# An encoder block on eight cores: six buffers for normalized rows, later x loads, and the last norm product split over two engines

## The chip, the cores and the metric

The kernel runs on all 8 cores of one Trainium2 chip. Each core computes one of the 8 sequences of the batch; nothing is exchanged between them. Cores 0 to 3 lie on one die, 4 to 7 on the other. The metric is the device time in microseconds (us) of the slowest core. Each core has a matrix engine (TensorE, PE), a vector engine (VectorE, DVE), ScalarE (ACT) and GpSimd (POOL); SyncE (SP) issues transfers. 16 DMA engines carry out what SP, ACT and POOL issue. Each engine takes its instructions in order, and semaphores order the engines among each other.

## The reference

What is computed, for one sequence of 2048 rows of 1024 (16 meta rows are put in front for the mixers):

```python
u = rmsnorm(h, norm1_g)
q, c, iq, ik, iw, pv, gates = split(u @ w_in)
attn = sparse_attention(...)            # top-256 keys of a chunk-causal indexer, shared latent
pool = multiscale_pool(pv, w_pool, pool_scale)
g_attn, g_pool = split(sigmoid(gates))
merged = g_attn * (attn @ w_branch_attn) + g_pool * (pool @ w_branch_pool)
h = h + merged @ w_out
u = rmsnorm(h, norm2_g)
h = h + hier_moe(u)                     # top-1 of 4 groups, top-2 of its 8 experts, hidden 256
out = rmsnorm(h, final_norm_g)          # meta rows dropped
```

The change is in the last three lines' surroundings: `h + merged @ w_out`, the second norm, and the last line.

## The kernel before

The program records each operation with the buffers it reads and writes (`pg.op`, `pg.dma`), and from these works out the semaphore waits; within an engine the order is that in which the code is written. The rows are cut into 16 tiles of 128 (`NT`). A tile of h is `hacc[:, j, :]`, 128 partitions of 1024 float32, in SBUF for the rest of the program.

Stages in order of time on the profiled core: projections and the indexer with sparse attention (to about 790 us), the branch products and gates giving `mergedT` (to 968), the **join stage** (968 to about 1076, with routing to 1098), the **expert stage** (to 1370), and the **final stage** (to the end). A barrier stands ahead of the join stage, none between it and the end of the final stage.

*Join stage.* Tiles are walked in the order `walk`: 12 to 15, 8 to 11, 0 to 7; t counts places in this walk. x of tiles 12 to 15 is loaded a stage earlier. At the start SP issues the gain, the routing constants, the twelve other x tiles (`load_x`) and the weights of experts 0 and 1 (`load_w`). In step t the code writes:

- `scale_rows(t-1)`: a reciprocal on DVE, then the norm product into a bf16 buffer `xn2[k]`. For even t-1 it is one DVE instruction (L1335). For odd it is a scaling on ACT (L1339) and a product with the gain on POOL (L1341).
- `join(t)`: twice 8 matmuls (L1314) into one of three PSUM banks, each followed by an add of x on DVE (L1319), then square and sum (L1323) and square root (L1325) on ACT.
- `flip(t-2)`: a write of `xn2[k]` to the table `u_rows` in device memory, issued by ACT; eight transpositions on PE (L1351) into a bank of their own, and a copy on ACT (L1355).
- `score_rows(t-3)`: eight small matmuls (L1364) and an add on DVE (L1368) give the router's logits. From t = 11 on, each step takes six operations of the first half's routing besides, nearly all on DVE.

There are two `xn2` buffers, in arena R0. The buffers `xg` for gathered rows (six of the same size, arena R2) are set to zero by POOL before the walk; in the expert stage `pull(i)` gathers rows of `u_rows` into them, leaving out rows whose index is out of bounds. The expert stage keeps four buffers of expert weights filled ahead of itself.

*Final stage.* `fetch(j)` brings two expert outputs per row (1 MB, SP), eight tiles ahead. `merge(j)` adds them to `hacc` with two DVE instructions (L1689) and takes square and root on ACT (L1692, L1695). `leave(j-1)` then takes the reciprocal on DVE (L1701), multiplies with reciprocal and gain on DVE (L1703) into one of six buffers `ofin`, and issues the output from ACT. Since `fetch(0)` to `fetch(7)` all claim the old buffers of the expert stage (list `moe`), the first `leave`, which claims them too, waits for the eighth fetch.

Of the kernel before, what the change touches and what calls it, by code (L numbers as in the profile page):

```python
# [9 lines left out]
BF16 = mybir.dt.bfloat16  # L10
ALU = mybir.AluOpType
AF = mybir.ActivationFunctionType
AX = mybir.AxisListType

P = 128
D = 1024
KC = 8
NT = 16
# [33 lines left out]
class Prog:  # L52
# [11 lines left out]
    def B(self, *key):  # L64
        b = self.bufs.get(key)
        if b is None:
            b = Buf(key)
            self.bufs[key] = b
        return b
# [191 lines left out]
def build(debug=None):  # L261
# [8 lines left out]
    x_d = din("x", [TX, D])  # L270
# [32 lines left out]
    pg = Prog(nc)  # L303
    B = pg.B

    with ExitStack() as es:
# [29 lines left out]
        def carve_at(nm, off, dtype, shape):  # L336
            save = cursor[nm]
            cursor[nm] = off
            ap = carve(nm, dtype, shape)
            assert (off + 63) // 64 * 64 == off  # L340
            cursor[nm] = save
            return ap
# [5 lines left out]
        banks_bf = [b.bitcast(BF16) for b in banks]  # L348
        PB = [B('psum', i) for i in range(8)]
# [3 lines left out]
        gbc = [carve('R0', F32, [P, D]) for _ in range(2)]  # L353
# [125 lines left out]
        for j in tiles:  # L479
            rows = 16 if j < 0 else 128  # L480
            col0 = 0 if j < 0 else 16 + 128 * j
            k = nxt('xt4', [0, 1, 2, 3])
# [236 lines left out]
        if stop_after >= 4:  # L719
# [11 lines left out]
            for m in range(4):  # L731
                bk = nxt('gen', allb)
                pg.op('pe', lambda e, bk=bk, m=m: e.transpose(
                    out=banks_bf[bk][:, 0:128], in_=wuk_bf[:, m * 128:(m + 1) * 128], identity=ident_bf),
                    reads=[B('wuk_bf'), B('ident_bf')], writes=[PB[bk]])
                for hp in range(2):
                    h = 2 * m + hp
                    pg.op('dve', lambda e, bk=bk, h=h, hp=hp: e.tensor_copy(
                        out=ukT_pad[64 * hp:64 * hp + 64, h, :], in_=banks_bf[bk][64 * hp:64 * hp + 64, 0:128]),
                        reads=[PB[bk], B('ukT_pad')], writes=[B('ukT_pad', h)])  # L740
# [434 lines left out]
        if run_tail:  # L1175
# [7 lines left out]
            for grp in range(4):  # L1183
# [57 lines left out]
        rstd2 = carve('R2', F32, [P, NT])  # L1241
# [10 lines left out]
        idx_s = carve('R2', I32, [P, 48])  # L1252
        wbuf = [carve_at('R0', 0, BF16, [P, 6144]), carve_at('R0', 12288, BF16, [P, 6144]),
                carve_at('R2', 16384, BF16, [P, 6144]), carve_at('R0', xt_off, BF16, [P, 6144])]
        xn2 = [carve_at('R0', 24576 + 2048 * i, BF16, [P, D]) for i in range(2)]
        uTs = [carve_at('R0', 28672 + 2048 * i, BF16, [P, KC, 128]) for i in range(2)]
        t32 = carve_at('R0', junk_off, F32, [P, D])
        sqj = carve_at('R3', 32768, BF16, [P, D])
# [24 lines left out]
        def load_w(x_):  # L1283
            load_gu_w(x_)
            load_d_w(x_)

        def load_x(j):
            pg.dma('sp', hacc[:, j, :], x_d[128 * j:128 * (j + 1), :], writes=[B('hacc', j, 0), B('hacc', j, 1)])

        if run_tail:  # L1290
            pg.dma('sp', gbc[1], g2_d.partition_broadcast(128), writes=[B('gbc', 1)])
            pg.dma('sp', rconst, croute_d, writes=[B('rconst')])
            for j in list(range(8, 12)) + list(range(0, 8)):
                load_x(j)
            load_w(0)
            load_w(1)
            for i in range(2):
                for q in range(3):
                    pg.op('pool', lambda e, i=i, q=q: e.memset(xg[i][q], 0.0), writes=[B('xg', i, q)])
            pg.op('pool', lambda e: e.tensor_copy(out=tri_bf, in_=rconst[:, 0:128]), reads=[B('rconst')], writes=[B('tri')])  # L1300
            pg.op('pool', lambda e: e.memset(ones_m, 1.0), writes=[B('ones_m')])
            pg.op('pool', lambda e: e.tensor_copy(out=iota_bf, in_=rconst[:, 128:384]), reads=[B('rconst')], writes=[B('iota')])
# [24 lines left out]
                      reads=[B('ssq', j), B('eps')], writes=[B('rs', j)])  # L1327

            def scale_rows(t):
                j, k = walk[t], t % 2  # L1330
                hb = [B('hacc', j, 0), B('hacc', j, 1)]
                pg.op('dve', lambda e: e.reciprocal(out=rstd2[:, j:j + 1], in_=rstd2[:, j:j + 1]),
                      reads=[B('rs', j)], writes=[B('rs', j)])
                if t % 2 == 0:
                    pg.op('dve', lambda e: e.scalar_tensor_tensor(  # L1335
                        out=xn2[k], in0=hacc[:, j, :], scalar=rstd2[:, j:j + 1], in1=gbc[1], op0=ALU.mult, op1=ALU.mult),
                        reads=hb + [B('rs', j), B('gbc', 1)], writes=[B('xn2', k)])
                else:
                    pg.op('act', lambda e: e.activation(out=t32, in_=hacc[:, j, :], func=AF.Identity, scale=rstd2[:, j:j + 1]),  # L1339
                          reads=hb + [B('rs', j)], writes=[B('t32')])  # L1340
                    pg.op('pool', lambda e: e.tensor_tensor(out=xn2[k], in0=t32, in1=gbc[1], op=ALU.mult),  # L1341
                          reads=[B('t32'), B('gbc', 1)], writes=[B('xn2', k)])

            def flip(t):
                j, k = walk[t], t % 2
                pg.dma('act', urow_d[128 * j:128 * (j + 1), :], xn2[k], reads=[B('xn2', k)], writes=[B('u_row', j)])

                def tps(e):
                    last = None
                    for kc in range(KC):  # L1350
                        last = e.transpose(out=banks_bf[TPB][:, kc * 128:(kc + 1) * 128],  # L1351
                                           in_=xn2[k].rearrange("t (p k) -> t k p", k=KC)[:, kc, :], identity=ident_bf)
                    return last
                pg.op('pe', tps, reads=[B('xn2', k), B('ident_bf')], writes=[PB[TPB]])
                pg.op('act', lambda e: e.copy(out=uTs[k], in_=banks_bf[TPB][:, 0:1024].rearrange("p (a b) -> p a b", a=KC)),  # L1355
                      reads=[PB[TPB]], writes=[B('uTs', k)])

            def score_rows(t):
                j, k = walk[t], t % 2
# [136 lines left out]
            for t in range(NT + 4):  # L1496
                if 1 <= t < NT + 1:
                    scale_rows(t - 1)
                if t < NT:
                    join(t)  # L1500
                if 2 <= t < NT + 2:
                    flip(t - 2)
                if 3 <= t < NT + 3:
                    score_rows(t - 3)
                if t >= NH + 3:
                    for _ in range(6):
                        if first_half:
                            first_half.pop(0)()
# [51 lines left out]
        def pull(i):  # L1560
            for q, col in ((0, 2 * i), (1, 2 * i + 1), (2, 32 + i)):
                pg.gather(xg[i % 2][q], urow_d, idx_g[:, col:col + 1], TX - 1,
                          reads=[B('idx_g')] + urows, writes=[B('xg', i % 2, q)])
        pull(0)
        pull(1)
        pg.branch_on(flag[0:1, 0:1], [B('flag')])
# [1 line left out]
        silm = [carve_at('R0', 24576 + 1536 * i, F32, [P, 2 * CAP]) for i in range(3)]  # L1568
        xTm = [carve_at('R3', 3072 * i, BF16, [P, KC, CAP]) for i in range(4)]
        ysb = [carve_at('R3', 12288 + 4096 * i, F32, [P, D]) for i in range(5)]  # L1570
        early = [B('xn2', k) for k in range(2)] + [B('uTs', k) for k in range(2)]
        late_r3 = [B('R3a')]

        def turn(i):
# [124 lines left out]
        def leave(j):  # L1699
            s = j % 6  # L1700
            pg.op('dve', lambda e: e.reciprocal(out=rstd2[:, j:j + 1], in_=rstd2[:, j:j + 1]),  # L1701
                  reads=[B('rs', j)], writes=[B('rs', j)])
            pg.op('dve', lambda e: e.scalar_tensor_tensor(  # L1703
                out=ofin[s], in0=hacc[:, j, :], scalar=rstd2[:, j:j + 1], in1=gbc[0], op0=ALU.mult, op1=ALU.mult),
                reads=[B('hacc', j, 0), B('hacc', j, 1), B('rs', j), B('gbc', 0)],
                writes=[B('ofin', s)] + (moe if j < 6 else []))
            pg.dma('act', out_d[128 * j:128 * (j + 1), :], ofin[s], reads=[B('ofin', s)], writes=[B('out', j)])

        for j in range(8):
# [203 lines left out]
```

How the kernel before makes its waits and increments, by code:

```python
        def stream(ename, h, ops, base, n):  # L209
            info = parts[n][1]
            for i, o in enumerate(ops):
                for t in o.waits:
                    if t[0] == 'c':
                        h.wait_ge(esem[t[1]], signo[n][t[1]][t[2]])
                    else:
                        s, val = info[t[1]]
                        h.wait_ge(dsem[s], val)
                if o.fn is None:
                    continue
                inst = o.fn(h)
                if o.dma is not None:
                    inst.then_inc(dsem[info[o.dma][0]], 16)
                elif base + i in signo[n][ename]:
                    inst.then_inc(esem[ename], 1)
```

## Time and profile before

| | us |
|---|---|
| median of 3 runs (lowest, highest) | 1492.72 (1492.47, 1503.7) |
| the profiled execution | 1493.79 |
| its span, core 7 | 1492.2 |
| span of the other cores | 1452.1 to 1488.1 |
| busy in the span: PE, DVE, ACT, POOL | 1066.1, 879.3, 738.9, 305.6 |

The span is the time from the first to the last instruction of the profiled core. The page's chain that ended last gives PE 45%, DVE 18%, ACT 8% and DMA 8% of it. A line such as L122, L125 or L130 is that of a helper that issues transfers; names such as R are the SBUF arenas, ps is PSUM, and `ACTq` or `SPq` marks the issue of a transfer on that engine's queue. A bracket in the timeline tells how long the engine was idle before an instruction and what released it.

### The profile page before, as it was taken

The page shows a single profiled execution, that of the slowest core. Times are in us where ns is not written, and L with a number is a line of the kernel's source. Part 1 is how long each engine was busy: PE and PEld are TensorE (multiplying, and loading weights), DVE is VectorE, ACT ScalarE, POOL GpSimd, SP SyncE. Part 2 cuts the span into 40 slices and gives each one's busy share as a digit, 9 for nine tenths or more (in the row PEclk, how much of TensorE's full clock was granted, in tenths as well). Part 3 has the DMA queues.
Part 4 walks back from the last instruction along what each step waited for, and adds up shares of the span by engine and source line. Part 5 has one row for each costly group of instructions (what it writes and reads, how often), then busy time and mean ns, then how long its engine had stood idle before and what let it go on. Part 6 is the DMA issues. An engine that isn't in the chain of part 4 may idle for free.

```text
span 1492.2 us, 23009 instructions; the slowest of 8 cores (1452.1 to 1492.2 us)
## 1 busy us (share of the span) xinstructions
PE 1066.1 (71%) x6606; PEld 546.1 (37%) x6606; DVE 879.3 (59%) x1812; ACT 738.9 (50%) x1387; POOL 305.6 (20%) x316
## 2 busy tenths in 40 slices
PE   2589667788888889999848999968547777776000
PEld 1345223333333334444423444424334544453000
DVE  3434699899999999999811344334632322322186
ACT  5733656677777778888743222235313323332132
POOL 2025402122121212221221000022123333332000
PEclk9999577889999999999988999989759998899555
DMA  9402554575868679999676220081237889985592
GB/s 195 113 1 29 63 58 58 71 97 74 97 72 98 81 83 108 112 105 104 90 97 136 30 29 1 1 296 50 85 109 247 274 270 293 288 297 174 190 350 107
DMA packets 76322, 187.73 MB, mean 126 GB/s; under 512 B 18792, under 2 KB 30568, under 8 KB 72096
## 3 DMA queue, kind: packets, MB, share of 16 engines
q0 software_dynamic: 51264, 87.55, 39.6%
q1 hardware_dynamic: 20320, 86.05, 18.8%
q10 hardware_dynamic: 4608, 12.58, 2.1%
q8 instruction: 59, 0.97, 0.3%
q14 instruction: 71, 0.58, 0.1%
HBM read 223.33 MB, written 88.08 MB: 209 GB/s over the span
## 4 chain that ended last, share of the span: by engine, by line
PE 45%; DVE 18%; issue 14%; ACT 8%; DMA 8%; another core or an unknown queue 3%; POOL 2%; DVEq 0%; ACTq 0%; SPq 0%; POOLq 0%
DVE R L961 9%; PE ps L1214 7%; PE ps L1608 5%; PE ps L1632 4%; DMA R<-y_rows 3%; PE ps L823 3%; PE ps L1020 2%; PE ps L1021 2%; PE ps L1038 2%; PE ps L1314 2%; PE ps L1039 2%; PE ps L623 2%; PE ps L1198 2%; PE ps L1206 2%
## 5 line engine op out<-in xcount | busy, mean ns | idle before, releaser
L961 DVE TENSOR_SCALAR_CACHE_REDUCE R<-R 128x272 bf16<-128x272 f32 (+14 forms) x240 | 342.2, 1426 | 11.6 <-DVE R L961 0.5
L1024 ACT ACTIVATE R<-ps,R 128x512 bf16<-128x512 f32 x304 | 209.1, 690 | 70.4 <-PE ps L1021 63.8
L813 ACT ACTIVATE R<-ps 128x400 bf16<-128x400 f32 (+14 forms) x352 | 159.3, 512 | 55.0 <-PE ps L808 53.5
L1038 PE MATMUL ps<-R 128*128 128x512 bf16 x304 | 120.2, 395 | 36.1 <-ACT R L1046 34.4
L1050 POOL TENSOR_TENSOR R<-R 128x512 bf16<-128x512 f32 x32 | 40.6, 1270 | 455.6 <-ACT R L1048 357.7
L1020 PE MATMUL ps<-R 128*128 128x512 bf16 x304 | 121.2, 399 | 7.4 <-DVE R L928 3.9
L823 PE MATMUL ps<-R 128*128 128x400 bf16 (+14 forms) x352 | 105.7, 379 | 26.1 <-POOL R L796 16.4
L1021 PE MATMUL ps<-R 128*128 128x512 bf16 x304 | 120.7, 397 | 0.0
L1039 PE MATMUL ps<-R 128*128 128x512 bf16 x304 | 120.2, 395 | 0.0
L1214 PE MATMUL ps<-R 128*128 128x512 bf16 x512 | 116.9, 382 | 0.0
L808 PE MATMUL ps<-R 32*128 32x400 bf16 (+14 forms) x352 | 71.9, 370 | 30.9 <-DVE R L928 14.9
L1632 PE MATMUL ps<-R 128*128 128x512 bf16 (+1 forms) x256 | 85.1, 448 | 11.6 <-ACT R L1641 9.3
L1608 PE MATMUL ps<-R 128*128 128x192 bf16 x1024 | 92.0, 249 | 0.7 <-DVE R L1594 0.7
L1608 PEld LDWEIGHTS ps<-R 128*128 128x128 bf16 x1024 | 84.7, 99 | 15.7 <-issue 15.4
L1615 DVE TENSOR_TENSOR R<-R,ps 128x384 bf16<-128x384 f32 x32 | 17.7, 555 | 109.7 <-remote 51.4
L130 POOL DMA_INDIRECT y_rows<-R x48 | 47.6, 992 | 161.9 <-DVE R L1644 64.7
L1226 DVE TENSOR_TENSOR R<-R,ps 128x512 f32<-128x512 f32 x32 | 22.0, 688 | 94.1 <-ACT R L1222 94.1
L1582 PE MATMUL ps<-R 128*128 128x128 bf16 x384 | 32.3, 240 | 61.7 <-ACT R L1590 52.0
L1214 PEld LDWEIGHTS ps<-R 128*128 128x128 bf16 x512 | 50.5, 99 | 61.6 <-issue 2.1
L1314 PE MATMUL ps<-R 128*128 128x512 bf16 x256 | 63.0, 402 | 10.5 <-DVE R L1319 8.1
L1641 ACT COPY R<-ps 128x512 f32<-128x512 f32 x64 | 37.3, 582 | 65.1 <-PE ps L1632 63.2
L1644 DVE COPY R<-ps 128x512 f32<-128x512 f32 x64 | 44.1, 690 | 42.0 <-PE ps L1632 40.9
(210 smaller groups left out, 1854.3 us busy)
## 6 DMA issues: line engine op xcount, KB each, us to landing
R<-expert_bf SPq DMA_DIRECT2D x32, 1024.0 KB
R<-x SPq DMA_DIRECT2D x32, 512.0 KB
expert_bf<-w_eg POOLq DMA_DIRECT2D x32, 512.0 KB, 12.1
expert_bf<-w_eu POOLq DMA_DIRECT2D x32, 512.0 KB
expert_bf<-w_ed POOLq DMA_DIRECT2D x32, 512.0 KB
R<-expert_bf SPq DMA_DIRECT2D x32, 512.0 KB
R<-y_rows SPq DMA_DIRECT2D x16, 1024.0 KB
out<-R ACTq DMA_DIRECT2D x16, 512.0 KB, 5.2
```

What stands on the lines that cost most here:

```text
L813: pg.op('act', lambda e, bx=bx, ri=ri: e.activation(out=rbuf[ri][:, 0:n], in_=banks[bx][:, 0:n], func=AF.Relu), reads=[PB[bx]], writes=[B( ...
L823: pg.op('pe', lambda e, h=h, ri=ri: e.matmul(banks[PSS][:, 0:n], lhsT=dg[:, h, :], rhs=rbuf[ri][:, 0:n], start=(h == 0), stop=(h == 7)), r ...
L961: pg.op('dve', lambda e: e.tensor_scalar(out=junkbf[:, 0:S], in0=sc[:, 0:S], scalar1=mids[:, n_ - 1:n_], scalar2=None, op0=ALU.is_ge, op1= ...
L1020: e.matmul(banks[bl][:, 0:512], lhsT=cnT[:, kc0:kc0 + 128], rhs=qrhs, start=True, stop=False)
L1021: return e.matmul(banks[bl][:, 0:512], lhsT=ident_bf, rhs=mrow, start=False, stop=True)
L1024: pg.op('act', lambda e: e.activation(out=pT[pi], in_=banks[bl][:, 0:512], func=AF.Exp, scale=ATTN_SCALE, bias=negsh[:, par:par + 1]), rea ...
L1038: e.matmul(banks[bO][:, 0:512], lhsT=ckeys[:, i, 0:128], rhs=pT[pi], start=first, stop=last_)
L1039: return e.matmul(banks[bS][:, 0:512], lhsT=ones_bf, rhs=pT[pi], start=first, stop=last_)
L1214: last = e.matmul(banks[bk][:, 0:512], lhsT=wt[:, kc, n4 * 128:(n4 + 1) * 128], rhs=uT[:, kc, c0:c0 + 512], start=(kc == 0), stop=(kc == K ...
L1314: last = e.matmul(banks[bk][:, 0:512], lhsT=mergedT[:, nn, 128 * j:128 * (j + 1)], rhs=w_out[:, nn, 512 * hh:512 * (hh + 1)], start=(nn == ...
L1608: last = e.matmul(banks[bk][:, CAP * fh:CAP * (fh + 1)], lhsT=w[:, c_:c_ + 128], rhs=xt_[:, kc, :], start=(kc == 0), stop=(kc == KC - 1))
L1632: last = e.matmul(banks[bk][lo:hi_, 0:512], lhsT=hd[:, f, t0:t1_], rhs=w[:, 4096 + 1024 * f + 512 * hh:4096 + 1024 * f + 512 * (hh + 1)], ...
```

## The change

In the join stage `xn2` becomes six buffers, which are the six `xg` buffers; their memsets are gone, and the first two `pull`s list the `xn2` buffers as written. Of x, only tiles 8 and 9 are asked for at the start. The others are asked for one at a time, tile `walk[t + 6]` once the first add of tile `walk[t]` is done; the weights of experts 0 and 1 are asked for in steps 6 and 9. In the final stage, the norm product of odd tiles becomes a scaling on ACT and a product in place on POOL.

```diff
-        xn2 = [carve_at('R0', 24576 + 2048 * i, BF16, [P, D]) for i in range(2)]
+        xn2 = [xg[i // 3][i % 3] for i in range(6)]
@@
-        def load_x(j):
-            pg.dma('sp', hacc[:, j, :], x_d[128 * j:128 * (j + 1), :], writes=[B('hacc', j, 0), B('hacc', j, 1)])
+        def load_x(j, after=()):
+            pg.dma('sp', hacc[:, j, :], x_d[128 * j:128 * (j + 1), :], reads=list(after), writes=[B('hacc', j, 0), B('hacc', j, 1)])
@@
-            for j in list(range(8, 12)) + list(range(0, 8)):
+            for j in range(8, 10):
                 load_x(j)
-            load_w(0)
-            load_w(1)
-            for i in range(2):
-                for q in range(3):
-                    pg.op('pool', lambda e, i=i, q=q: e.memset(xg[i][q], 0.0), writes=[B('xg', i, q)])
@@ scale_rows
-                j, k = walk[t], t % 2
+                j, k = walk[t], t % 6
@@ flip (uTs, the copy's target, stays at two buffers: ku)
-                j, k = walk[t], t % 2
+                j, k, ku = walk[t], t % 6, t % 2
@@ the walk
                     join(t)
+                    if t + 6 < NT:
+                        load_x(walk[t + 6], [B('hacc', walk[t], 0)])
+                    if t in (6, 9):
+                        load_w(t // 3 - 2)
@@ pull
-                          reads=[B('idx_g')] + urows, writes=[B('xg', i % 2, q)])
+                          reads=[B('idx_g')] + urows, writes=[B('xg', i % 2, q)] + ([B('xn2', 3 * i + q)] if i < 2 else []))
@@
-        early = [B('xn2', k) for k in range(2)] + [B('uTs', k) for k in range(2)]
+        early = [B('uTs', k) for k in range(2)]
@@ leave
-            pg.op('dve', lambda e: e.scalar_tensor_tensor(
-                out=ofin[s], in0=hacc[:, j, :], scalar=rstd2[:, j:j + 1], in1=gbc[0], op0=ALU.mult, op1=ALU.mult),
-                reads=[B('hacc', j, 0), B('hacc', j, 1), B('rs', j), B('gbc', 0)],
-                writes=[B('ofin', s)] + (moe if j < 6 else []))
+            hb = [B('hacc', j, 0), B('hacc', j, 1)]
+            al = moe if j < 6 else []
+            if j % 2 == 0:
+                pg.op('dve', lambda e: e.scalar_tensor_tensor(
+                    out=ofin[s], in0=hacc[:, j, :], scalar=rstd2[:, j:j + 1], in1=gbc[0], op0=ALU.mult, op1=ALU.mult),
+                    reads=hb + [B('rs', j), B('gbc', 0)], writes=[B('ofin', s)] + al)
+            else:
+                pg.op('act', lambda e: e.activation(out=ofin[s], in_=hacc[:, j, :], func=AF.Identity, scale=rstd2[:, j:j + 1]),
+                      reads=hb + [B('rs', j)], writes=[B('ofin', s)] + al)
+                pg.op('pool', lambda e: e.tensor_tensor(out=ofin[s], in0=ofin[s], in1=gbc[0], op=ALU.mult),
+                      reads=[B('ofin', s), B('gbc', 0)], writes=[B('ofin', s)])
```

Lines behind the removed ones have numbers lower by five, and in the final stage by one: L1319 becomes L1314, L1335 becomes L1330, L1692 becomes L1691.

The order on SP's queue at the start of the join stage. `expert_bf` are the weights in pairs of a 1 MB and a 0.5 MB load:

```order
 L122 DMA R<-c_route 128x560
-L122 DMA R<-x 128x1024 x12
+L122 DMA R<-x 128x1024 x9
 L122 DMA R<-expert_bf 128x4096
 L122 DMA R<-expert_bf 128x2048
+L122 DMA R<-x 128x1024 x3
 L122 DMA R<-expert_bf 128x4096
 L122 DMA R<-expert_bf 128x2048
```

Three x loads (for t = 7, 8, 9) now stand behind the weights of expert 0; which of the others wait for an add is not in these rows.

ScalarE's order in the final stage, from the square of tile 2 on. First the kernel before: L1692 is the square, L1695 the root.

```order
L1692 ACTIVATE R<-R 128x1024
L1695 ACTIVATE R<-R 128x1
L122 DMA out<-R 128x1024
L1692 ACTIVATE R<-R 128x1024
L1695 ACTIVATE R<-R 128x1
```

And the kernel changed, from the same place (L1691 is the square, L1694 the root, L1709 the new scaling of tile 1):

```order
L1691 ACTIVATE R<-R 128x1024
L1694 ACTIVATE R<-R 128x1
L1709 ACTIVATE R<-R 128x1024
L122 DMA out<-R 128x1024
L1691 ACTIVATE R<-R 128x1024
L1694 ACTIVATE R<-R 128x1
L122 DMA out<-R 128x1024
```

The scaling stands between a tile's root and the previous tile's output issue, in every second step; the last one stands alone ahead of the last issue. GpSimd's order, at the start of the join stage and at the end of the program:

```order
-L1299 MEMSET R 128x1024 x6
-L1300 CAST R<-R 128x128
-L1301 MEMSET R 128x128
-L1302 CAST R<-R 128x256
-L1341 TENSOR_TENSOR R<-R 128x1024 x8
+L1295 CAST R<-R 128x128
+L1296 MEMSET R 128x128
+L1297 CAST R<-R 128x256
+L1336 TENSOR_TENSOR R<-R 128x1024 x8
...
 L130 DMA y_rows<-R 4096x1024 x11
+L1711 TENSOR_TENSOR R<-R 128x1024 x8
```

Six memsets are gone, and eight products are new behind the last scatter.

## Rows read from the trace of the kernel before

**Rows 1.** Busy time by stretch (length; engines busy; PE clock, DMA share, GB/s).

```profile
982.40:994.70 12.30, 4.38 (x33) 2.02 (x30) 2.16 (x4) 2.06 (x4) 2.03 (x1) 0.85 1.01 319
...
1008.00:1023.80 15.80, 14.28 (x102) 7.14 (x99) 7.08 (x15) 9.25 (x14) 2.38 (x1) 0.89 0.14 51
...
1419.70:1480.00 60.30, 0.00 (x0) 0.00 (x0) 56.43 (x59) 20.21 (x42) 0.00 (x0) 0.50 0.73 261
```

**Rows 2.** Timeline, the first stall: start, duration, engine, line [idle before <-releaser].

```profile
983.26 0.38 ACTq L122 DMA_DIRECT2D u_rows<-R  x1
...
985.73 1.89 PE L1314 MATMUL ps<-R 128*128 128x512 bf16 x8
992.70 1.28 DVE L1335 SCALAR_TENSOR_TENSOR R<-R 128x1024 bf16<-128x1024 f32 x1 [8.89 <-DMA u_rows<-R]
...
994.73 3.36 PE L1314 MATMUL ps<-R 128*128 128x512 bf16 x8 [7.12 <-DVE R L1319]
...
1004.43 2.34 POOL L1341 TENSOR_TENSOR R<-R 128x1024 bf16<-128x1024 f32 x1 [20.00 <-DMA u_rows<-R]
...
1006.91 1.05 PE L1351 MATMUL ps<-R 128*128 128x128 bf16 x8 [4.41 <-POOL R L1341]
...
1013.82 3.61 PE L1314 MATMUL ps<-R 128*128 128x512 bf16 x16
```

**Rows 3.** Timeline, a later stretch of the join stage.

```profile
1023.83 3.61 PE L1314 MATMUL ps<-R 128*128 128x512 bf16 x16
...
1027.35 1.28 DVE L1335 SCALAR_TENSOR_TENSOR R<-R 128x1024 bf16<-128x1024 f32 x1 [1.65 <-DMA u_rows<-R]
...
1032.81 0.68 PE L1351 MATMUL ps<-R 128*128 128x128 bf16 x8 [1.22 <-ACT R L1355]
...
1043.36 3.61 PE L1314 MATMUL ps<-R 128*128 128x512 bf16 x16
...
1047.51 3.69 PE L1314 MATMUL ps<-R 128*128 128x512 bf16 x16
```

**Rows 4.** Timeline of GpSimd and VectorE, late in the join stage.

```profile
1053.98 2.35 POOL L1341 TENSOR_TENSOR R<-R 128x1024 bf16<-128x1024 f32 x1 [7.61 <-ACT R L1339]
1054.23 2.71 DVE L1436 TENSOR_TENSOR R<-R 128x256 f32<-128x256 f32 x2
...
1057.05 0.43 DVE L1439 TENSOR_TENSOR R<-R 128x256 bf16<-128x256 f32 x1
```

**Rows 5.** Timeline of GpSimd and VectorE, early in the program.

```profile
126.26 2.30 DVE L652 SCALAR_TENSOR_TENSOR R<-R 128x2057 bf16<-128x2057 f32 x1 [2.23 <-POOL R L645]
128.48 1.85 DVE L656 TENSOR_TENSOR R<-R 128x7 f32<-128x7 f32 x1
...
127.31 3.00 POOL L639 TENSOR_TENSOR R<-R 128x1023 f32<-128x1023 f32 x1
...
135.47 1.89 POOL L639 TENSOR_TENSOR R<-R 128x1023 f32<-128x1023 f32 x1 [0.21 <-POOL R L645]
```

**Rows 6.** Timeline of the final stage, first tiles and last issues.

```profile
1419.67 1.28 DVE L1703 SCALAR_TENSOR_TENSOR R<-R 128x1024 f32<-128x1024 f32 x1 [31.45 <-DMA R<-y_rows]
1420.87 2.67 DVE L1689 SCALAR_TENSOR_TENSOR R<-R 128x1024 f32<-128x1024 f32 x2
...
1423.63 1.06 ACT L1692 ACTIVATE R<-R 128x1024 bf16<-128x1024 f32 x1 [33.85 <-DVE R L1701]
1423.72 1.28 DVE L1703 SCALAR_TENSOR_TENSOR R<-R 128x1024 f32<-128x1024 f32 x1
...
1424.88 0.29 ACT L1695 ACTIVATE R<-R 128x1 f32<-128x1 f32 x1
...
1477.69 2.16 ACTq L122 DMA_DIRECT2D out<-R  x2
```

**Rows 7.** Two ScalarE lines: count, min/median/max in ns, first and last start.

```profile
L1339 ACT ACTIVATE R<-R x8: 1149/1153/1159, 980.8 to 1067.7; 128x1024 f32<-128x1024 f32 x8
...
L1355 ACT COPY R<-ps x16: 1005/1012/1012, 983.7 to 1074.4; 128x1024 bf16<-128x1024 bf16 x16
```

More of the change, by code:

```diff
@@ L1354, in flip @@
                 pg.op('pe', tps, reads=[B('xn2', k), B('ident_bf')], writes=[PB[TPB]])
-                pg.op('act', lambda e: e.copy(out=uTs[k], in_=banks_bf[TPB][:, 0:1024].rearrange("p (a b) -> p a b", a=KC)),
-                      reads=[PB[TPB]], writes=[B('uTs', k)])
+                pg.op('act', lambda e: e.copy(out=uTs[ku], in_=banks_bf[TPB][:, 0:1024].rearrange("p (a b) -> p a b", a=KC)),
+                      reads=[PB[TPB]], writes=[B('uTs', ku)])
             def score_rows(t):
```

## The prediction

> **What bounds the kernel now.** I read the stage windows first, then the timeline of core 7 (the slowest, and the one profiled) in the two stages that the change touches, then what each wait there was released by. Times are microseconds from the span's start.
>
> The join stage runs from 968.6 to about 1076 and has two regimes. While x and the first weights are streaming in, the 16 DMA engines are full: their share is 1.01 in 982.4 to 994.7, against 0.14 in 1008.0 to 1023.8 [rows 1]. In that flood the first write of normalized rows is issued at 983.26, and the norm product of tile 2 (L1335), which needs the same buffer back, starts only at 992.70, after 8.89 of idle time. The vector engine runs in order, so the adds that free PSUM banks stand behind it, and TensorE stops for 7.12. The GpSimd product of tile 3 waits in the same way until 1004.43, and TensorE waits another 4.41 for it, then runs its next eight matmuls cold (3.36 for eight, against 1.89 before) [rows 2]. After 1008 the write lands sooner, but each even product still waits 1.65, and it passes the delay on by way of the ScalarE copy to TensorE (1.22); two pairs of tiles take from 1023.83 to 1043.36, so 9.77 a pair [rows 3].
>
> The final stage is bound by the vector engine: 56.43 busy of 60.3 [rows 1]. Its cycle for one tile is two merges (2.67 with their gap), a reciprocal and the norm product (1.28); the products of neighbouring tiles start at 1419.67 and 1423.72, so 4.05 a tile. ScalarE needs only 1.54 a tile there, from 1423.63 to the end of the square root at 1425.17, and GpSimd nothing [rows 6]. The chain begins at 1419.67 because the first product waits for the eighth fetch; the change leaves that wait alone, since tile 0 is even and keeps its place and its list of old buffers.
>
> **Part one: six buffers, x asked for late, no memsets.** The six memsets are GpSimd work ahead of its first product and nobody waits for them: 0. Six buffers remove the wait for the write from two tiles back, at all places. What comes next in line I worked out from tile 4 on. Its matmuls start at 985.73 as before. Product 2 runs at 983.8 instead of 992.7, so the adds of tile 3 are done at 986.4 and tile 4 ends at 989.2. From there the slowest loop goes through ScalarE: square and root 1.54 [rows 6], issue 0.38 [rows 2], copy 1.01 and, for odd tiles, the scaling 1.15 [rows 7], where a transposition waits for the previous copy. A product on GpSimd takes 2.35 [rows 4] and also holds up the even tile's vector product for about 0.6. This gives tile 5 at 990.5, tile 6 at 995.1 and tile 7 at 1000.0, against 1013.82 in the trace [rows 2]: 13.8 gained. From there a pair costs 4.55 plus 4.65, 9.2 instead of 9.77, over two and a half pairs 1.4. From tile 11 on the vector engine is filled by the routing steps of the first half, and no more of the pace comes through; but it reaches that section one removed wait of 1.65 earlier, less what the slower chain takes, which I put at 1.3. **Sum of part one: 16.5 gained.** The lower bound takes the early stalls alone without the cold matmuls, less a ScalarE loop that is a little longer than I think: 12. The upper bound is TensorE's own pace, 4.15 a tile as between 1043.36 and 1047.51 where it waited for nothing [rows 3], from tile 4 to 11: about 20.
>
> The x loads are costed at nothing. A load now goes out when the add of the tile six places ahead is done, so it has 6 times 4.6, or 27.6, before its own add. The first write under a full queue took 9.4 (983.26 to 992.70) [rows 2]. Behind the load at step 6 stand 1.5 MB of expert weights and at step 9 again 1.5 MB; at the 319 GB/s of the full window [rows 1] that is 4.7 for a load that stands behind them. If that cover were gone, the adds, and so PSUM, would wait.
>
> **Part two: the last product split.** For odd tiles the vector engine loses 1.28 less overlap, 1.20. In exchange ScalarE gets 1.15 [rows 7] and GpSimd 2.35, and the output's issue on ScalarE's queue now waits for GpSimd. Queued behind it are the next tile's square and root, on which the next reciprocal depends.
>
> What decides is whether the two engines can run side by side. In the trace they can't when both read two SBUF operands. GpSimd's product of 2.35 starts at 1053.98; a pair of vector TENSOR_TENSORs of 256 columns (0.43 each alone) starts at 1054.23 and takes 2.71 [rows 4]. The first ended only once GpSimd was done. The other way round, a SCALAR_TENSOR_TENSOR runs from 126.26 to 128.56, and a GpSimd TENSOR_TENSOR that starts at 127.31 takes 3.00, where the same form takes 1.89 alone. The vector instruction of seven columns queued next took 1.85, up to GpSimd's end [rows 5]. So each blocks the other, and a waiting GpSimd instruction gets its turn ahead of the vector engine's next one. The merges and products of the final stage are all of the form that blocks. The Trainium skill says the same (SBUF — State Buffer, "Who interferes with whom"): a vector instruction with two SBUF inputs contends with a GpSimd one that reads SBUF, and the loser blocks fully. By that rule a split of this kind adds GpSimd's time to the vector engine's; without it, it would take 1.20 off every second tile. The trace agrees with the rule.
>
> A pair of tiles is then, on the vector engine, 8.1 - 1.2 + 2.2 = 9.1 (2.2 and not 2.35, since a blocked vector instruction gets going some 0.15 before GpSimd's printed end). ScalarE's chain in a pair is 1.54 + 0.1 + 1.15 + 0.1 + 2.35 + 0.1 + 0.4 + 1.54 + 0.4 = 7.7, which fits in 9.1. From the first merge of tile 2 (1420.87 in the trace) to the issue of the last output there are now six pairs of 9.1, so 54.6, and a last one of about 14.8: two merges end 5.4 in, GpSimd's product 13 runs from 5.6 or 6.9, the output issue, square and root of tile 15 come after it (about 10.7), then reciprocal, scaling 1.15, product 2.35 and issue. That is 69.4. The trace has 58.6, to the second issue at about 1479.5 [rows 6]. **Sum of part two: 10.8 lost**, with bounds of 8 (GpSimd's turn partly in gaps) and 12.5.
>
> The 8 and 12.5 assume that GpSimd with float32 output takes 2.35, as with bf16 output. The row of 1.89 is float32 to float32 [rows 5], so nothing speaks for much more.
>
> **Sum.** 16.5 gained and 10.8 lost make 5.7 gained. The profiled execution took 1493.79 (span 1492.2), the median of the runs is 1492.72, a difference of 1.1 that I leave aside. 1492.7 - 5.7 = **1487.0**. What follows the last output's issue is untouched, and the expert stage between the two changed ones shifts as a whole.
>
> **Rivals.**
> - *No mutual blocking in the final stage.* Then the pair is bound by ScalarE's chain, 7.7: six of them and a last one of 14.1 make 60.3, still 1.7 more than the trace, because the last tile is odd and its longer way lies open. The net is 14.8 gained: 1478. For it speaks only that no row shows this exact pair of forms with both at 1024 columns. Chance 0.06.
> - *GpSimd is starved.* If the vector engine's instructions leave no gap, GpSimd comes only when the vector engine waits for the root behind the blocked issue. Then a pair costs 6.9 + 2.35 + 0.45 + 1.54, 11.2, or 3.1 more than now; seven of these and the tail of 2.3 lose 24, net 7.5 lost: 1500. It decides if GpSimd loses more than two turns in a pair. Against it stands the row of 127.31, where it got in at once. Chance 0.04.
> - *x late.* If loads need over 27.6, the gain of part one goes and part two stays: 1503. It needs three times the longest landing in the rows. Chance 0.04.
> - *Part one pays more*, because ScalarE's loop is shorter than worked out: 20 gained and 9 to 10.8 lost, 1482. Chance 0.10.
> - The forecast itself, 1487, with its own range of 1481 to 1493: chance 0.76.
>
> **How the numbers follow.** The forecast and the case of a better part one hold 0.86. To reach 8 in 10 with the uncertainty of both bounds I take the edge of the first rival and a little over the forecast's own upper end: 1478 to 1495. A change of under 1% (14.9) is about what a measurement of this kernel can't tell from none. Faster by more needs the first rival or both lucky bounds: 0.09. Slower by more than 1% needs starvation or late x at their worst: 0.04. The rest is 0.87.
>
> **What would show it.** In the profile after: no wait of a product for a u_rows write; TensorE's stalls of 7.12 and 4.41 gone; the stage from its first matmul to the last logits add some 16 shorter. In the final stage vector rows of about 3.5 instead of 1.28 wherever GpSimd's product runs, a pair of 9.1, and about 70 from tile 2's merge to the last issue. It would be wrong if the GpSimd rows and the vector rows overlap at full length, if the scaling on ScalarE waits for something other than its reciprocal, or if adds wait for x.

## The result

The changed kernel takes 1479.27 us (median of 4 runs, 1476.2 to 1482.97), the kernel before 1492.6; the ratio is 0.990, 95% interval 0.9853 to 0.9946. The forecast was 5.7 gained, the profiled executions differ by 10.8 (1493.79 to 1482.97), the medians by 13.3. So the sign and the place were right, and the size was about half of what came. Medians, ratios and intervals, here and below, leave out the executions in which the cores of one die ran at a lower clock and finished some per cent later.

The profile after is again that of core 7, span 1481.4. On that core, between fixed points of the program:

| stretch on core 7, us | before | after | forecast change | measured change |
|---|---|---|---|---|
| start to first matmul of the join stage | 968.6 | 968.6 | 0 | 0 |
| join stage and routing (to the last cast of the router) | 129.3 | 110.9 | -16.5 | -18.4 |
| from there to the first product of the final stage | 321.8 | 321.3 | 0 | -0.5 |
| first product of the final stage to the end | 72.5 | 80.6 | +10.8 | +8.1 |
| span | 1492.2 | 1481.4 | -5.7 | -10.8 |

The same two stretches on all eight cores: join and routing 125.8 to 131.8 before, 110.9 to 111.6 after; the final stage 72.5 to 72.8 before and 80.6 on every core after.

The last row ends with a closing stretch, from the landing of the last output to the end of the span. It is the same on all eight cores of a kernel, within 0.05, and differs between kernels; why is open: 10.1 before, 9.9 after, and 8.5 to 10.5 in the kernels below. The program does no computing in it, so the final stage is also read from its first product to the issue of the last output: 59.8 before, 68.0 after, 8.2 more, on every core.

First the join stage. In the windows of the changed kernel (columns as in [rows 1]) the engines that stood still in the same stretch are at work, at full clock, and the DMA engines carry their load evenly:

```profile
982.40:994.70 12.30, 11.12 (x90) 5.97 (x88) 7.30 (x13) 7.87 (x13) 4.34 (x2) 1.00 0.59 191
994.70:1008.00 13.30, 12.95 (x98) 6.82 (x97) 7.30 (x16) 9.46 (x15) 2.35 (x1) 1.00 0.82 273
```

TensorE is busy for 11.12 of 12.30, where it was 4.38 [rows 1]. The timeline of the changed kernel from tile 4 on:

```profile
983.23 0.35 ACTq L122 DMA_DIRECT2D u_rows<-R  x1
...
983.88 1.59 DVE L1330 SCALAR_TENSOR_TENSOR R<-R 128x1024 bf16<-128x1024 f32 x1
...
985.67 3.61 PE L1309 MATMUL ps<-R 128*128 128x512 bf16 x16
...
989.65 0.69 PE L1346 MATMUL ps<-R 128*128 128x128 bf16 x8 [0.37 <-ACT R L1350]
...
999.05 3.61 PE L1309 MATMUL ps<-R 128*128 128x512 bf16 x16
...
1003.20 3.61 PE L1309 MATMUL ps<-R 128*128 128x512 bf16 x16
...
1007.72 3.61 PE L1309 MATMUL ps<-R 128*128 128x512 bf16 x16
```

Product 2 starts at 983.88, where it started at 992.70 [rows 2]. Tile 7 starts at 999.05 instead of 1013.82 [rows 2]. From there tiles follow in 4.15 and 4.52, a pair in 8.67, where it was 9.77 [rows 3]. What is left of waiting is a few tenths for ScalarE's copy.

Now the final stage of the changed kernel, from its first product to the last issue:

```profile
1400.82 1.28 DVE L1705 SCALAR_TENSOR_TENSOR R<-R 128x1024 f32<-128x1024 f32 x1 [32.12 <-DMA R<-y_rows]
1402.02 2.67 DVE L1688 SCALAR_TENSOR_TENSOR R<-R 128x1024 f32<-128x1024 f32 x2
...
1406.22 1.13 ACT L1709 ACTIVATE R<-R 128x1024 f32<-128x1024 f32 x1
...
1407.50 2.33 POOL L1711 TENSOR_TENSOR R<-R 128x1024 f32<-128x1024 f32 x1 [57.11 <-ACT R L1709]
1407.53 3.40 DVE L1705 SCALAR_TENSOR_TENSOR R<-R 128x1024 f32<-128x1024 f32 x1
1409.91 0.34 ACTq L122 DMA_DIRECT2D out<-R  x1
1410.36 1.06 ACT L1691 ACTIVATE R<-R 128x1024 bf16<-128x1024 f32 x1 [3.01 <-POOL R L1711]
1410.84 2.66 DVE L1688 SCALAR_TENSOR_TENSOR R<-R 128x1024 f32<-128x1024 f32 x2
...
1416.32 2.34 POOL L1711 TENSOR_TENSOR R<-R 128x1024 f32<-128x1024 f32 x1 [6.48 <-ACT R L1709]
...
1454.92 2.66 DVE L1688 SCALAR_TENSOR_TENSOR R<-R 128x1024 f32<-128x1024 f32 x2
...
1466.44 2.34 POOL L1711 TENSOR_TENSOR R<-R 128x1024 f32<-128x1024 f32 x1 [3.71 <-ACT R L1709]
1468.86 0.34 ACTq L122 DMA_DIRECT2D out<-R  x1
```

The even tile's product, 1.28 alone, takes 3.40 when GpSimd's product has started 0.03 before it, and ends 1.1 after GpSimd's end: this is what it would do if it did its own work only then. A pair takes 8.82 (GpSimd from 1407.50 to 1416.32), where two tiles took 8.1 [rows 6]. From the merge of tile 2 at 1402.02 to the last issue at 1468.86 it is 66.8, against 58.6.

### The profile page after: what moved, and what is told of

It reads as the page before. It is cut to its first block, busy times and chain, and to the rows that moved or that the text cites. A ratio compares the mean times of both kernels' runs of the same rounds, so it can differ in the third digit from the quotient of the medians.

```text
span 1481.4 us, 23028 instructions; the slowest of 8 cores (1438.8 to 1481.4 us)
## 1 busy us (share of the span) xinstructions
PE 1064.9 (72%) x6606; PEld 549.1 (37%) x6606; DVE 886.1 (60%) x1804; ACT 748.1 (50%) x1395; POOL 318.1 (21%) x318
## 4 chain that ended last, share of the span: by engine, by line
PE 42%; DVE 21%; issue 15%; ACT 8%; DMA 7%; another core or an unknown queue 3%; POOL 1%; DVEq 0%; ACTq 0%; SPq 0%; POOLq 0%
DVE R L961 11%; PE ps L1214 8%; PE ps L1607 5%; PE ps L1631 4%; DMA R<-y_rows 3%; PE ps L1309 2%; PE ps L623 2%; PE ps L823 2%; PE ps L1198 2%; PE ps L1206 2%; PE ps L1038 2%; PE ps L1020 2%; PE ps L1021 2%; PE ps L1039 2%
## 5 line engine op out<-in xcount | busy, mean ns | idle before, releaser
L1038 PE MATMUL ps<-R 128*128 128x512 bf16 x304 | 120.9, 398 | 33.5 <-ACT R L1046 32.3
L1020 PE MATMUL ps<-R 128*128 128x512 bf16 x304 | 122.1, 401 | 6.4 <-DVE R L928 3.0
L1021 PE MATMUL ps<-R 128*128 128x512 bf16 x304 | 121.3, 399 | 0.0
L1039 PE MATMUL ps<-R 128*128 128x512 bf16 x304 | 120.4, 396 | 0.0
L1214 PE MATMUL ps<-R 128*128 128x512 bf16 x512 | 116.7, 381 | 0.0
L1631 PE MATMUL ps<-R 128*128 128x512 bf16 (+1 forms) x256 | 81.3, 433 | 11.7 <-ACT R L1640 10.2
L1222 ACT ACTIVATE R<-ps 128x512 f32<-128x512 f32 x32 | 19.1, 597 | 88.8 <-PE ps L1214 88.8
```

Of the source, the lines that this page charges most:

```text
L1020: e.matmul(banks[bl][:, 0:512], lhsT=cnT[:, kc0:kc0 + 128], rhs=qrhs, start=True, stop=False)
L1021: return e.matmul(banks[bl][:, 0:512], lhsT=ident_bf, rhs=mrow, start=False, stop=True)
L1038: e.matmul(banks[bO][:, 0:512], lhsT=ckeys[:, i, 0:128], rhs=pT[pi], start=first, stop=last_)
L1039: return e.matmul(banks[bS][:, 0:512], lhsT=ones_bf, rhs=pT[pi], start=first, stop=last_)
L1214: last = e.matmul(banks[bk][:, 0:512], lhsT=wt[:, kc, n4 * 128:(n4 + 1) * 128], rhs=uT[:, kc, c0:c0 + 512], start=(kc == 0), stop=(kc == K ...
L1631: last = e.matmul(banks[bk][lo:hi_, 0:512], lhsT=hd[:, f, t0:t1_], rhs=w[:, 4096 + 1024 * f + 512 * hh:4096 + 1024 * f + 512 * (hh + 1)], ...
```

## The experiments

In the tables of this section "join" is the stretch from the first matmul of the join stage to the end of routing, "final" that from the first product of the final stage to the end, and "to the last issue" that from the same product to the issue of the last output; where no core is named, the mean of the eight is given. Whole times scatter by several us between executions, so the stretches carry most verdicts. The kernels ran in three groups, each on a chip of its own, with the kernel before beside them: first the two halves, six buffers and late loads (before: 1492.07), then write-only, bystander and early claims (1487.91), then three buffers and late weights (1504.65, a single execution). Ratios are to the kernel before of the same group.

**The halves apart.** The join-only kernel keeps the old product in the final stage, the other one keeps the old join stage:

```diff
 e1_join_only: the changed kernel, but in leave
-            if j % 2 == 0: ... else: ... (the split)
+            pg.op('dve', lambda e: e.scalar_tensor_tensor(out=ofin[s], ...))
 e2_final_only: the kernel before, but in leave the split
```

> The join-stage half of the change alone (six buffers, late x, no memsets); the final stage keeps its product on the vector engine. Theory A (the two halves add up: the join stage gains 18.4 as in the trace of the changed kernel, the split product costs 8.2): the first merge of tile 2 starts near 1402, the last output issue follows 58.6 later, and the time is 1471 to 1475, faster than the changed kernel by about 8. Rival B (the split product costs nothing at the end, because the last outputs or the fetches bound the final stage anyway): the time is that of the changed kernel, 1479.

> The final-stage half alone: odd tiles scaled on ScalarE and multiplied on GpSimd, join stage as before. Theory A: 8.2 slower than the kernel before, 1500 to 1502, with a pair of tiles at 8.8 in place of 8.1 and vector products of 3.4 wherever GpSimd's runs. Rival B: within 2 of the kernel before.

The join-only kernel took 1473.44 (ratio 0.986, interval 0.9761 to 0.9959), the final-only one 1503.21 (1.007, interval 1.003 to 1.0111). Final: 73.2 and 81.2, against 72.6 before and 80.6 with the whole change. To the last issue: 60.2 and 68.05, against 59.8 and 68.0. The final-only kernel shows the same pair of rows as the changed one:

```profile
1444.89 2.34 POOL L1712 TENSOR_TENSOR R<-R 128x1024 f32<-128x1024 f32 x1 [6.48 <-ACT R L1710]
1444.91 3.41 DVE L1706 SCALAR_TENSOR_TENSOR R<-R 128x1024 f32<-128x1024 f32 x1
```

So the split costs 7.8 to 8.2 up to the last issue, wherever it stands, and rival B falls. The join-only kernel should then have been 8 faster than the changed one; it is 5.8 faster by the medians and 6 by the ratios, whose intervals overlap. Its join is 113.4, not 111.3, which accounts for the rest. On core 7 the first 40 matmuls took 10.48 in the join-only kernel (granted clock 0.85 in the first 11.7) and 8.79 in the changed one (1.00):

```profile
965.32 10.48 PE L1309 MATMUL ps<-R 128*128 128x512 bf16 x40 [2.53 <-DVE R L1230]
...
965.30:977.00 11.70, 10.74 (x42) 4.43 (x43) 3.84 (x6) 2.73 (x4) 0.77 (x3) 0.85 0.59 204
```

But that isn't the whole of it: on cores 1 to 5 of the changed kernel the first 40 took 10.48 as well, and their join is still 111.4 to 111.6. Against those the join-only kernel loses its 2 at the end of the walk. In the middle of its last tile but one TensorE waits for an add, and the last sixteen matmuls are slower. First core 7 of the join-only kernel, then core 1 of the changed one:

```profile
1030.85 1.89 PE L1309 MATMUL ps<-R 128*128 128x512 bf16 x8 [1.16 <-DVE R L1314]
...
1040.11 5.86 PE L1309 MATMUL ps<-R 128*128 128x512 bf16 x16
```

```profile
1033.40 4.86 PE L1309 MATMUL ps<-R 128*128 128x512 bf16 x16
```

The code is the same in both up to the end of routing. What shifts the late add, and why the clock falls on some cores and not on others, is open. The wait ahead of the first matmul, 2.53 in the join-only kernel and 2.43 in the changed one, doesn't decide it: cores with 10.48 and cores with 8.79 both show 2.43 in the changed kernel.

**Buffers or loads.** Two kernels take the join half apart, both with the old product at the end:

```diff
 e3_six_buffers: the join-only kernel with all loads at the start
+            for j in list(range(8, 12)) + list(range(0, 8)):
+                load_x(j)
+            load_w(0)
+            load_w(1)
 e4_late_x: the kernel before (two buffers, memsets) with the loads of the change
+                    if t + 6 < NT:
+                        load_x(walk[t + 6], [B('hacc', walk[t], 0)])
+                    if t in (6, 9):
+                        load_w(t // 3 - 2)
```

> Six buffers for normalized rows (and so no memsets), with all x loads and the weights of experts 0 and 1 asked for at the start as before; final stage as before. Theory C (the buffers carry the gain; the flooded queue then harms nobody, since a write has six tiles to land): no product waits for a write, the join stage is as short as with both, time as the join-only kernel within 2. Rival D (the late loads carry it): the writes still land 9 to 10 late and something else waits, gain under 6.

> Late x and weight loads alone, two buffers and the memsets kept; final stage as before. Theory C: the first writes land in 2 to 4 instead of 9 and the stalls of 7.1 and 4.4 on TensorE mostly go, but each even product keeps its wait of about 1.65, so the gain is 10 to 13, time 1480 to 1483. Rival D (late loads carry all of it): gain 18, 1474. Rival E (two buffers serialize at any queue length): gain under 4.

Six buffers alone took 1476.62 (0.9893, interval 0.9797 to 0.999), join 111.3: all of the gain. No product waits for a write of `u_rows` on any core, although the queue is as full as before, and although single writes took up to 10.5 to land on cores 4 to 7 and up to 20.8 on cores 0 to 3. This kernel lacks the memsets too, but they aren't what it gains by: on core 7 the first GpSimd product, behind the memsets, starts at 982.08 before and at 982.04 in the changed kernel. Late loads alone took 1490.89 (0.9987, interval 0.9944 to 1.003), join 130.5 against 128.4 before: none of it. That is where my expectation was wrong: theory C had 10 to 13 for the late loads. The first wait did shrink, but others grew in its place:

```profile
984.32 0.34 ACTq L122 DMA_DIRECT2D u_rows<-R  x1
...
987.25 1.28 DVE L1333 SCALAR_TENSOR_TENSOR R<-R 128x1024 bf16<-128x1024 f32 x1 [2.38 <-DMA u_rows<-R]
...
1006.50 2.34 POOL L1339 TENSOR_TENSOR R<-R 128x1024 bf16<-128x1024 f32 x1 [9.39 <-DMA u_rows<-R]
...
1012.70 1.28 DVE L1333 SCALAR_TENSOR_TENSOR R<-R 128x1024 bf16<-128x1024 f32 x1 [6.59 <-DMA u_rows<-R]
```

These are from core 5 of the late-loads kernel. Product 2 waits 2.38 instead of 8.89 [rows 2]. But at 1003.7 the weights of expert 0 enter the queue, and a product waits 6.59; in the kernel before, the queue was nearly empty by then (DMA share 0.14 [rows 1]) and the wait 1.65 [rows 3]. Over the stage of core 5 the vector engine's waits for writes are 19.0, where the kernel before has 16.2 on that core, and GpSimd's are 47.3 instead of 32.1.

To see whether the weights alone did this, they were put behind the walk; and to see how deep the buffers must be, the join-only kernel was run with three:

```diff
 e10_late_x_late_w: e4_late_x without its load_w in the walk
             load_w(2)   ->   load_w(0); load_w(1); load_w(2)
 e9_three_buffers: the join-only kernel
-        xn2 = [xg[i // 3][i % 3] for i in range(6)]
+        xn2 = [xg[0][i] for i in range(3)]
-                j, k = walk[t], t % 6
+                j, k = walk[t], t % 3
```

> Late x with two buffers, and the weights of experts 0 and 1 asked for only behind the walk (the late-x kernel asked for them in steps 6 and 9 and kept the stretch at 129 to 132). Theory J (the weights were the flood that kept the late-x kernel slow): the stretch falls to 116 to 122. Theory K (with two buffers a product waits for its write at any traffic; the x loads in small portions are enough): 124 to 130.

> The join-only kernel with three buffers for normalized rows instead of six (late x as in the change). Read by the stretch from the first matmul of the join stage to the end of routing: 129 before with two, 111.4 with six. Theory C (a write has one tile of 4.3 more to land than with two; writes of this stage land in 2 to 7.5 on core 5 and 7): most of it, 112 to 116. Rival: a write needs the full depth, 120 or more.

Join 126.0 without the weights (123.0 to 128.5 by core), so theory K: against late loads with the weights in the walk it is some 4 shorter, a difference between single profiled executions on two chips, and with two buffers the products wait for their writes without the weights too. With three buffers it is 114.7. The writes of `u_rows` were waited for as follows (engine and line that waited, us in all, number of waits), first on core 1 of the late-weights kernel, then on core 1 of the one with three buffers:

```profile
  POOL R L1339: 35.1, 3
  DVE R L1333: 15.6, 5
```

```profile
  DVE R L1330: 5.3, 3
```

Their single executions took 1476.12 (three buffers) and 1490.8 (late weights), against 1504.65 for the kernel before on the same chip. Three buffers with late loads carry four fifths of the gain (13.7 of 17.1), six the rest. Three buffers with all loads at the start weren't tried.

**What the final stage pays for.** In the first of two kernels GpSimd's product is replaced by work of the same length that reads nothing; it leaves out the gain of the odd tiles. In the second, GpSimd products that nobody waits for are added to the join-only kernel:

```diff
 e5_write_only: the changed kernel
-                pg.op('pool', lambda e: e.tensor_tensor(out=ofin[s], in0=ofin[s], in1=gbc[0], op=ALU.mult), ...)
+                for n in (1024, 1024, 420):
+                    pg.op('pool', lambda e, n=n: e.memset(wide[:, 0:n], 1.0), reads=[B('gbc', 0)], writes=[B('ofin', s), B('wide')])
 e8_bystander: the join-only kernel
+            if j % 2 == 1:
+                pg.op('pool', lambda e: e.tensor_tensor(out=wide, in0=gbc[0], in1=gbc[0], op=ALU.mult),
+                      reads=[B('rs', j), B('gbc', 0)], writes=[B('wide')])
```

> The changed kernel with GpSimd's product of the odd tiles replaced by three memsets of a scratch tile, 0.95 + 0.95 + 0.43 long, ordered in the same way (after ScalarE's scaling, before the output's issue). It leaves out the gain factor of the odd tiles. GpSimd then reads nothing from SBUF. Theory A (the 8 us that the final stage lost are VectorE and GpSimd excluding each other): vector products back at 1.28, a pair bound by ScalarE's chain at 7.7 instead of 8.8, final stage from its first product to the end 74 to 75 instead of 80.6. Rival F (the loss is ScalarE's queue waiting for GpSimd, exclusion is hidden behind it): pair stays at 8.8, 80.6.

> The join-only kernel with eight GpSimd products added in the final stage that nobody needs (gain times gain into a scratch tile, released by the root of each odd tile). Nobody waits for them. Theory A: each holds the vector engine up by 2.1, so a pair goes from 8.1 to 10.2 and the final stage from 72.6 to about 89. Rival F (an unneeded GpSimd product costs nothing): 72.6 to 73.2 as before.

With writes only, the final stage is 73.1 to 73.3, and the timeline of its core 6 shows the two engines side by side:

```profile
1413.76 2.59 POOL L1713 MEMSET R<- 128x1024 f32 x3 [5.09 <-ACT R L1710]
1413.79 1.28 DVE L1706 SCALAR_TENSOR_TENSOR R<-R 128x1024 f32<-128x1024 f32 x1
...
1416.43 0.34 ACTq L122 DMA_DIRECT2D out<-R  x1
1416.87 1.06 ACT L1692 ACTIVATE R<-R 128x1024 bf16<-128x1024 f32 x1 [3.28 <-POOL R L1713]
...
1418.50 0.16 DVE L1701 RECIPROCAL R<-R 128x1 f32<-128x1 f32 x1 [0.85 <-ACT R L1695]
...
1421.42 1.28 DVE L1706 SCALAR_TENSOR_TENSOR R<-R 128x1024 f32<-128x1024 f32 x1
```

The product is back at 1.28 although GpSimd has started 0.03 before it, just as in the changed kernel. The pair takes 7.63 (1413.79 to 1421.42), bound by ScalarE, whose next square waits 3.28 for GpSimd and whose root the reciprocal waits for. Final is 7.5 shorter than in the changed kernel, but 1.3 of that is the closing stretch (8.6 against 9.9). To the last issue it is 61.95 against 68.0. So of the 8.2 that the split cost, exclusion while both engines read is 6.1, and the other 2.1 is left without it: the pairs are shorter (7.6, two of them 8.0 and 8.2 on core 7), but the last tile is odd, and its longer way through ScalarE and GpSimd lies open. Without exclusion the split would still have lost that: 61.95 against 59.8 before and 60.2 in the join-only kernel. The whole time was 1473.74 (0.9902, interval 0.9866 to 0.9938).

The bystander products cost 10.0 by the whole stretch (final 83.2) and 11.8 to the last issue (72.0 against 60.2), with nobody waiting for them; whole time 1486.53 (0.996, interval 0.9931 to 0.9989). The expectation was 16. It took 2.1 for each; but this product, gain times gain, takes 1.89 and not 2.34, seven of the eight lie ahead of the last vector product, and each of them adds 1.6 to 1.7. From core 5:

```profile
1424.55 2.67 DVE L1689 SCALAR_TENSOR_TENSOR R<-R 128x1024 f32<-128x1024 f32 x2
...
1427.39 1.28 DVE L1703 SCALAR_TENSOR_TENSOR R<-R 128x1024 f32<-128x1024 f32 x1
1427.49 2.93 POOL L1708 TENSOR_TENSOR R<-R 128x1024 f32<-128x1024 f32 x1 [6.79 <-DVE R L1701]
1428.60 4.30 DVE L1689 SCALAR_TENSOR_TENSOR R<-R 128x1024 f32<-128x1024 f32 x2
```

Here the product began first, GpSimd waited 1.04 for it (2.93 instead of 1.89), and then the merge that was next in line waited for GpSimd (4.30 instead of 2.67). A waiting GpSimd instruction does get its turn ahead of the vector engine's next, as in [rows 5]. The Trainium skill (SBUF — State Buffer, "Who interferes with whom") says that such a vector instruction contends with a GpSimd one that reads SBUF and not with one that only writes it; the 3.40 of the changed kernel and the 1.28 beside memsets agree with both halves of that.

**A version that beats both.** The first product of the final stage idles for 31.45 behind the eighth fetch [rows 6], since each fetch claims all old buffers. Here the output buffers are claimed by six one-column memsets before the first fetch:

```diff
 e6_claim_early: the join-only kernel; e7_claim_early_split: the same in the changed kernel
+        for s in range(6):
+            pg.op('dve', lambda e, s=s: e.memset(ofin[s][:, 0:1], 0.0), writes=[B('ofin', s)] + moe)
         for j in range(8):
             fetch(j)
-                writes=[B('ofin', s)] + (moe if j < 6 else []))
+                writes=[B('ofin', s)])
```

> The join-only kernel, with the six output buffers claimed from the expert stage by six one-column memsets before the first fetch, so that the first product no longer waits for the eighth fetch. Theory G (fetches of 1 MB land every 5.1, and a tile of vector work is 4.05, so the final stage runs at the fetches' pace): merges and products follow each landing, the last fetch lands some 82 to 85 after the first is issued, and the end comes 15 to 25 earlier than with the join-only kernel. Rival H (output writes and fetches share the same bandwidth, 24 MB at 362 GB/s, and the wait only moved work): gain under 5.

> The same early claim in the changed kernel, so with the split product. Theory G: a pair takes 10.2 of fetching, more than the 8.8 of the split pair, so the split costs only the tail, 2 to 4 more than the kernel with the early claim alone. Rival I: the split costs its 8 here too.

With the early claim the kernel takes 1454.11 (0.9773, interval 0.9723 to 0.9824); from the first merge to the last issue it is 82.4 as a mean of the cores, where the join-only kernel has 98.2. So 15.8 come from one wait (14.9 on cores 0 to 3 alone). The timeline of its core 5:

```profile
1373.13 2.67 DVE L1688 SCALAR_TENSOR_TENSOR R<-R 128x1024 f32<-128x1024 f32 x2 [1.49 <-DMA R<-y_rows]
...
1378.43 2.67 DVE L1688 SCALAR_TENSOR_TENSOR R<-R 128x1024 f32<-128x1024 f32 x2 [1.17 <-DMA R<-y_rows]
...
1381.28 1.28 DVE L1702 SCALAR_TENSOR_TENSOR R<-R 128x1024 f32<-128x1024 f32 x1
...
1383.96 2.67 DVE L1688 SCALAR_TENSOR_TENSOR R<-R 128x1024 f32<-128x1024 f32 x2 [1.40 <-DMA R<-y_rows]
```

Merges follow the landing of their fetch, 5.3 and 5.5 apart, and products no longer wait. With the split on top it is 1471.5 (0.9877, interval 0.9802 to 0.9951), and the same stretch 88.1: the split costs 5.7 here (4.8 on cores 0 to 3), more than the tail that theory G allowed and less than rival I's 8. The traces show why. The fetches set the pace only in part of the stage. With the early claim alone the merges of tiles 8 to 12 wait for no fetch on core 3 and start 4.0 to 4.1 apart, which is the vector engine's own pace; with the split, on core 5, pairs of tiles from there on take 8.8 to 8.9.

## Why the prediction was right or wrong

- *What bounds each stage.* Right. The two TensorE stalls of 7.12 and 4.41 were waits for a write from two tiles back; six buffers alone took them away.
- *x loads late: 0.* Right as a price: no add of the changed kernel waits for x on any core. The margin was read from core 7 alone, where a write took 9.4; on cores 0 to 3 writes took up to 23.0 to land, near the cover of 27.6. As a cause it was worth nothing either: with six buffers, loads in front or late give 111.3 both. I had not separated the two in the prediction, and my later expectation of 10 to 13 for the late loads was wrong.
- *Part one, 16.5: the size was off, 18.4 came.* The step that failed is "a pair costs 4.55 plus 4.65, 9.2". It measured 8.67, of 4.15 and 4.52. The 4.15 is TensorE's own pace, so ScalarE's loop, taken as the slowest, doesn't set it: it was drawn too long. A pair thus gained 1.10 where the forecast had 0.57, or 2.8 instead of 1.4 over two and a half. Tile 7 came at 999.05 instead of 1000.0, 1.0 more. The product of place 10, just ahead of the routing steps, came at 1018.42 against 1037.12, 18.7 earlier, and 18.4 of it went through to the end of routing.
- *Part two, 10.8: the mechanism was right, the size was off, 8.2 came.* The step that failed is "8.1 - 1.2 + 2.2 = 9.1": the pair was 8.82, which is 1.7 over six pairs. A product after a blocked start took 3.40, so the exclusion added 2.12 and not 2.2. And an odd tile saved the vector engine 1.39 and not 1.20: from its reciprocal to the next merge it took 1.46 before (1431.55 to 1433.01 on core 7) and 0.07 after (1413.42 to 1413.49), since the pause between reciprocal and product is gone with the product. The last pair was 13.9 instead of 14.8: the product of tile 14 and GpSimd's of tile 13 began together (1460.41 and 1460.40), so GpSimd's ran from 5.5 on, near the earlier of the two starts that the forecast allowed.
- *The sum.* Two terms of opposite sign were each off by 2 to 3, in the same direction. That is 11% and 24% of the terms, but 4.5 on a net of 5.7. The profiled pair shows 10.8 where 5.7 was forecast. The medians show 13.3; the rest of 2.5 is in no trace and is within the scatter of the executions of one kernel, 6.8 (1476.2 to 1482.97). No term explains that rest.
- *The rivals.* Without mutual blocking I had a pair of 7.7 and 1.7 lost to the last issue; the write-only kernel shows 7.6 for most pairs and 2.1, so what the rival would give was drawn about rightly; it isn't what happened. Starvation did not occur.
- The range of 1478 to 1495 holds the median, by its lower edge, and the chance of 0.87 for a change under 1% stands at its edge too: the ratio is 0.990, and its interval reaches to both sides of that bound. The forecast's own range (1481 to 1493) missed. It used bounds of 12 to 20 and 8 to 12.5, and both terms came close to the bound on the fast side.

## What to carry to other kernels

Where a write from an in-order engine's product must land before its buffer is used again, give it buffers for the latency in the full queue, and try that before spreading the loads: six buffers were worth 17.1 us of the join stage here with the loads in front or spread, three of them 13.7 with the loads spread, and spreading the loads with two buffers nothing. Don't split an elementwise product of two SBUF tiles between VectorE and GpSimd when VectorE is busy with the same kind of work: of GpSimd's 2.34 us, 2.12 were added to VectorE's time. And count the last tile, whose longer way nothing hides: even without exclusion the split lost 2.1 us. Before you compare ends of two kernels, look whether the stretch behind the last output is the same. When a net is the difference of two large terms, give it the errors of the terms, not a share of itself.

## What was not expected of the hardware

- A GpSimd product of 1024 columns took 2.34 with a scaled tile and the gain as inputs, and 1.89 with the gain as both inputs (the bystander kernel). That there are two tiles can't be the reason by itself: an earlier product of the kernel before (L796, 1024 columns) reads two different tiles, each with elements repeated, and took 1.89 to 1.93. What makes the difference is open.
- The stretch from the end of routing to the first merge, the same code on every core, took 253 to 261 on cores 0 to 3 and 272 to 284 on cores 4 to 7 in the kernel before and the join-only kernel. In those of the three-buffer and late-weights kernels, on another chip, it was the other die that was slow (272 to 285 on cores 0 to 3, 254 to 262 on 4 to 7). What makes a die slow there was not tried.
- The first 40 matmuls of the join stage took either 8.79 or 10.48 on the same core number with identical code ahead of them, and the last 16 anything from 4.5 to 6.1.
- Writes of `u_rows`, 256 KB each, had a median landing of 2.0 to 3.2 on cores 4 to 7 of the kernel before and of 11.7 to 12.3 on cores 0 to 3, with the longest at 23.0. In the three-buffer kernel, on the other chip, it was cores 4 to 7 that had the long ones (12.5 to 13.1).
